# Both mixer tails as one stage per tile, with layer norm's sums over channel chunks on GpSimd

## The reference, cut to what matters

```python
# layer 0, after the depthwise convolution (u)
u = jax.nn.silu(layernorm(u, ln_g, ln_b))        # mean and variance over the 1024 channels
y = u @ pw2_w + pw2_b
x = x + g1 * y
# layer 1, after the scans (o = o_forward + o_backward, 4 heads of 256)
on = o * lax.rsqrt(jnp.mean(o * o, axis=-1, keepdims=True) + EPS)   # per head
x = x + g1 * ((on * head_g * jax.nn.silu(gate)) @ w_o)
# both: what the experts and the router read
h = rmsnorm(x, norm_g[i, 1]) * (1 + sc2) + sh2
g_logits, inner = h @ wg + bg, h @ wr + br       # 4 groups, 32 experts: 36 columns
```

## Time and profile before

| | us |
|---|---|
| median of 3 runs | 3279.66 |
| the profiled execution | 3279.33 |
| its span | 3277.7 |
| PE, DVE, ACT, POOL busy | 2565.8, 2039.8, 1393.5, 403.9 |
| first DMA of `conv_out` | 543.20 |
| first product of `conv_out` | 586.44 |
| last DVE instruction of `conv_out` starts | 728.41 |
| `route` of layer 0: first DMA, first maximum | 790.17, 815.90 |
| first product of `gla_output` | 2368.4 |
| `route` of layer 1: first maximum | 2541.31 |

### The profile page before, as it was taken

One profiled execution on the slowest core, in us unless ns is written; L12 is line 12 of the kernel. 1 busy time (PEld: TensorE's weight loads), 2 busy tenths in 40 slices (PEclk: granted clock), 3 DMA queues, 4 the chain that ended last, 5 costly groups with the idle time before them and its releaser, 6 DMA issues. The chain is left out here.

```text
span 3277.7 us, 41009 instructions
## 1 busy us (share of the span) xinstructions
PE 2565.8 (78%) x13258; PEld 2060.5 (63%) x13258; DVE 2039.8 (62%) x1900; ACT 1393.5 (43%) x1431; POOL 403.9 (12%) x447
## 2 busy tenths in 40 slices
PE   4587771984499999999925998968494499999980
PEld 0466661773388888888714886757482388888860
DVE  2479997545657777588353002348454688888865
ACT  0310001423356676577332113334312377777752
POOL 0000001000000101010051000055100110101004
PEclk8688895995699999999957999989796699999995
DMA  8354432114578899799473211013543599999966
GB/s 299 99 181 145 140 104 84 52 68 162 184 280 317 319 324 349 265 384 388 167 274 128 74 48 46 14 60 123 200 160 141 195 380 382 389 386 392 395 245 218
DMA packets 297487, 701.32 MB, mean 214 GB/s; under 512 B 22500, under 2 KB 49796, under 8 KB 297374
## 3 DMA queue, kind: packets, MB, share of 16 engines
q1 hardware_dynamic: 258802, 570.75, 48.3%
q0 software_dynamic: 22656, 75.60, 6.5%
q10 hardware_dynamic: 15936, 53.75, 4.3%
HBM read 610.01 MB, written 91.06 MB: 214 GB/s over the span
## 5 line engine op out<-in xcount | busy, mean ns | idle before, releaser
L1388 DVE TENSOR_TENSOR moe_w_lo<-moe_w_raw,moe_w_hi 128x2048 fp32r<-128x2048 f32 x384 | 862.0, 2286 | 83.6 <-ACT moe_w_hi L1317 47.5
L1317 ACT ACTIVATE moe_w_hi<-moe_w_raw 128x2048 fp32r<-128x2048 f32 x384 | 713.9, 1908 | 58.4 <-issue 37.9
L99 PE MATMUL moe_pg<-moe_w_hi,moe_xt_hi 128*128 128x512 f32 x592 | 243.9, 412 | 11.2 <-DVE moe_xt_lo L1399 5.9
L99 PE MATMUL moe_py<-moe_w_hi,moe_at_hi 128*128 128x512 f32 x592 | 241.9, 409 | 11.8 <-DVE moe_w_lo L1388 8.2
L100 PE MATMUL moe_pg<-moe_w_lo,moe_xt_hi 128*128 128x512 f32 x592 | 237.1, 401 | 0.0
L101 PE MATMUL moe_pg<-moe_w_hi,moe_xt_lo 128*128 128x512 f32 x592 | 237.0, 400 | 0.0
L100 PE MATMUL moe_py<-moe_w_lo,moe_at_hi 128*128 128x512 f32 x592 | 235.4, 398 | 0.0
L101 PE MATMUL moe_py<-moe_w_hi,moe_at_lo 128*128 128x512 f32 x592 | 234.9, 397 | 0.0
L101 PE MATMUL moe_pu<-moe_w_hi,moe_xt_lo 128*128 128x512 f32 x592 | 234.6, 396 | 0.0
L99 PE MATMUL moe_pu<-moe_w_hi,moe_xt_hi 128*128 128x512 f32 x592 | 234.4, 396 | 0.0
L100 PE MATMUL moe_pu<-moe_w_lo,moe_xt_hi 128*128 128x512 f32 x592 | 234.4, 396 | 0.0
(11 more groups left out here) (311 smaller groups left out, 5599.7 us busy)
## 6 DMA issues: line engine op xcount, KB each, us to landing
moe_w_raw<-in_moe_w SPq DMA_DIRECT2D x384, 1024.0 KB, 9.9
taps_ada_w<-in_ada_w SPq DMA_DIRECT2D x40, 1024.0 KB, 6.9
scratch_experts_out<-moe_y ACTq DMA_DIRECT2D x57, 512.0 KB, 6.4
norm_x<-scratch_residual SPq DMA_DIRECT2D x28, 512.0 KB, 3.3
scan_v<-scratch_gla_values SPq DMA_DIRECT2D x20, 512.0 KB, 4.1
scratch_experts_in<-norm_h POOLq DMA_DIRECT2D x18, 512.0 KB, 3.0
comb_x<-scratch_residual SPq DMA_DIRECT2D x18, 512.0 KB, 5.5
ada_w<-in_ada_w SPq DMA_DIRECT2D x4, 2048.0 KB, 29.2
```

Of the source, the lines that this page charges most:

```text
L99: pe.matmul(out, xh, wh, start=start, stop=False)
L1317: act.activation(hi[m][:, cut, :], raw[m][p][:, cut, :], ACT.Copy).then_inc(s(f"{m}_hi{h}"), 1)
L1388: dve.tensor_tensor(lo[m][:, cut, :], raw[m][p][:, cut, :], hi[m][:, cut, :].bitcast(F32), ALU.subtract).then_inc(s(f"{m}_lo{h}"), 1)
```

## The change

`conv_out` and `gla_output` now do per tile what `normalise` and the first part of `route` did, and those are gone from behind them. Both are written out over the tiles without hardware loops, as a software pipeline: iteration n works on the front of tile n+2, the product of tile n, the residual and norm of tile n-1 and the logits of tile n-2. `x` of a tile is normalised while it lies in SBUF; `h` is transposed and split for one tile at a time, and the logits are computed with the tokens stationary and the 36 router columns moving, so that they come out with tokens on partitions and are kept in `lg`, in the order that `route` wants. The slots of the raw weights serve as `y` and `h` once the weights are split. The stores of `x` and `h` are issued by SP. In `conv_out` GpSimd adds the 8 chunks (4+4, 2+2, 1+1) of `vt` and of its square, and PE does one product with the 1/1024 matrix for each. `dev`, `sq` and Silu work in place on `vt`, with one `sq` buffer. `route` only loads its five tables and starts with the first maximum. The diff, cut:

On GpSimd and PE in `conv_out`:

```diff
+                def over_chunks(src, dst, name):
+
+                    if added[0]:
+                        pool.wait_ge(s("halved"), added[0])
+                    pool.tensor_tensor(quads[:, :, :], src[:, 0:KC // 2, :], src[:, KC // 2:KC, :], ALU.add)\
+                        .then_inc(s("halved"), 1)
+                    pool.wait_ge(s("halved"), added[0] + 1)
+                    pool.tensor_tensor(pairs[:, :, :], quads[:, 0:2, :], quads[:, 2:4, :], ALU.add)\
+                        .then_inc(s("halved"), 1)
+                    pool.wait_ge(s("halved"), added[0] + 2)
+                    pool.tensor_tensor(dst[:, :], pairs[:, 0, :], pairs[:, 1, :], ALU.add).then_inc(s(name), 1)
+                    added[0] += 2
+
+                def total_of(t):
+                    if t not in tiles:
+                        return
+                    if t >= 2:
+                        pool.wait_ge(s("mean"), t - 1)
+                    over_chunks(vt[:, :, cols(t)], total[t % 2], "totalled")
+
+                def power_of(t):
+                    if t not in tiles:
+                        return
+                    pool.wait_ge(s("squared"), t + 1)
+                    if t >= 2:
+                        pool.wait_ge(s("var"), t - 1)
+                    over_chunks(sq, power[t % 2], "powered")
...
+                for n in range(-2, TILES):
+                    if n < 0:
+                        weight(4 * (n + 2) + 1)
+                    power_of(n + 2)
+                    if n < 0:
+                        weight(4 * (n + 2) + 3)
+                    total_of(n + 3)
 
             @block.tensor
             def _(pe):
-                def average(what, b, i, t0):
-
+                pe.wait_ge(s("mean_w"), 16)
+
+                def mean_of(t):
+                    if t not in tiles:
+                        return
+                    if t:
+                        pe.wait_ge(s("root"), t)
+                    pe.wait_ge(s("totalled"), t + 1)
+                    pe.matmul(mean, mean_w[:, :], total[t % 2][:, :], start=True, stop=True).then_inc(s("mean"), 1)
+
+                def variance_of(t):
+                    if t not in tiles:
+                        return
+                    pe.wait_ge(s("powered"), t + 1)
+                    pe.matmul(var, mean_w[:, :], power[t % 2][:, :], start=True, stop=True).then_inc(s("var"), 1)
...
+                def route_scores(t):
+                    if t not in tiles:
+                        return
+                    pe.wait_ge(s("ht_lo"), t + 1)
+                    if t == 0:
+                        pe.wait_ge(s("router_ready"), 2)
+                    else:
+                        pe.wait_ge(s("lg"), t)
+                    for k in range(KC):
+                        last = product3(pe, logits[:, 0:router.WIDTH], ht.hi[:, k, :], ht.lo[:, k, :],
+                                        router.w.hi[:, k, :], router.w.lo[:, k, :], k == 0, k == KC - 1)
+                    last.then_inc(s("scored"), 1)
+
+                for n in range(-2, TILES + 2):
+                    mean_of(n + 2)
+                    product(n, 0)
+                    variance_of(n + 2)
+                    route_scores(n - 2)
+                    product(n, 1)
+                    turn(n - 1)
```

ACT and DVE in `conv_out`:

```diff
+                for n in range(-2, TILES + 2):
+                    if n < 0:
+                        for k in range(2):
+                            weight(4 * (n + 2) + k)
+                    square(n + 2)
+                    if n < 0:
+                        for k in range(2, 4):
+                            weight(4 * (n + 2) + k)
+                    if n == 0:
+                        router.high(act)
+                    rms(n - 1)
+                    root_of(n + 2)
+                    silu(n + 2)
+                    row_high(n - 1)
+                    act_high(n + 2)
 
...
+                for n in range(-2, TILES + 2):
+                    bias_in(n - 1)
+                    deviation(n + 2)
+                    row_low(n - 2)
+                    residual(n - 1)
+                    if n < 0:
+                        for k in (0, 2):
+                            weight(4 * (n + 2) + k)
+                    act_low(n + 1)
+                    if n == 0:
+                        router.low(dve)
+                        dve.wait_ge(s("tables"), 16 * 9)
+                        for st in (CTX, LAT):
+                            dve.scalar_tensor_tensor(scale[:, st, :], scale[:, st, :], 1.0, gain[:, :],
+                                                     ALU.add, ALU.mult).then_inc(s("scale_ready"), 1)
+                        dve.wait_ge(s("scale_ready"), 2)
+                    norm(n - 1)
+                    spread(n + 2)
+                    keep_logits(n - 2)
+                dve.wait_ge(s("lg"), TILES)
         ph.close()
 
```

SP in `conv_out`, and in `route` SP's tables with the start of DVE:

```diff
+                    load_x(t)
+                router.load(sp)
+                for t in tiles:
+                    sp.wait_ge(s("x_ready"), t + 1)
+                    sp.dma_start(d.xs[t * P:(t + 1) * P, :], x[t % 2][:, :]).then_inc(s(f"x_stored{t % 2}"), 16)
+                    sp.wait_ge(s("h_ready"), t + 1)
+                    sp.dma_start(d.hd[t * P:(t + 1) * P, :], h[t % 2]).then_inc(s(f"hd_stored{t % 2}"), 16)
+                    if t + 2 in tiles:
+                        load_x(t + 2)
...
+                for dst, src in ((iota[:, :], d.iota), (before[:, :], d.before), (ones[:, :], d.ones),
+                                 (token[:, :], d.token), (next_e[:, :], d.next_expert)):
                     sp.dma_start(dst, src).then_inc(s("loaded"), 16)
...
+                dve.wait_ge(s("loaded"), 80)
                 first_max(lg[:, :, 0:GROUPS], GROUPS, gm[:, :], gsel[:, :, :])
```

`gla_output`: SP's start, then PE, ACT and DVE:

```diff
+                load_o(0)
+                sp.dma_start(head_g[:, :], d.head_g[0, :].partition_broadcast(P)).then_inc(s("head_g"), 16)
+                sp.dma_start(ident[:, :], d.ident).then_inc(s("ident"), 16)
                 weights.load(sp)
...
+                def turn_h(t):
+                    if t not in tiles:
+                        return
+                    pe.wait_ge(s("h_ready"), t + 1)
+                    pe.wait_ge(s("ot_lo"), min(t + 3, LAT_TILES))
+                    if t:
...
+                for n in range(-1, LAT_TILES + 2):
+                    product(n, 0)
+                    turn_o(n + 1)
+                    route_scores(n - 2)
+                    product(n, 1)
+                    turn_h(n - 1)
...
+                for n in range(-2, LAT_TILES + 1):
+                    if n == -2:
+                        for k in range(2):
+                            weight(k)
+                    head_root(n + 2)
+                    if n == -2:
+                        for k in range(2, 6):
+                            weight(k)
+                    rms(n - 1)
+                    ot_high(n + 1)
+                    if n == -1:
+                        for k in range(6, KC):
+                            weight(k)
+                    if n == 0:
+                        router.high(act)
+                    row_high(n - 1)
 
...
+                for n in range(-2, LAT_TILES + 2):
+                    gated(n - 1)
+                    row_low(n - 2)
+                    residual(n - 1)
+                    front(n + 2)
+                    norm(n - 1)
+                    if n == -2:
+                        weight(0)
+                    head_norm(n + 2)
+                    if n == -2:
+                        weight(2)
+                        weight(4)
+                    ot_low(n + 1)
+                    if n == -1:
+                        weight(6)
+                    if n == 0:
...
+                    keep_logits(n - 2)
```

More of the change, by code:

```diff
@@ L704, in _ @@
[L704 to L712 removed]
+                sp.dma_start(gain[:, :], d.norm_g[0, 1, :].partition_broadcast(P)).then_inc(s("tables"), 16)
@@ L714, in _ @@
+                for b in range(2):
+                    sp.wait_ge(s(f"x_stored{b}"), 16 * (TILES // 2))
+                    sp.wait_ge(s(f"hd_stored{b}"), 16 * (TILES // 2))
             @block.gpsimd
             def _(pool):
[L716 to L722 removed]
@@ new lines, in rms @@
+                def rms(t):
+                    if t not in tiles:
+                        return
+                    act.wait_ge(s("x_ready"), t + 1)
+                    if t == 0:
+                        act.wait_ge(s("scale_ready"), 2)
+                    act.activation(junk[:, :], x[t % 2][:, :], ACT.Square, accum_out=stat[:, t, 0:1])\
+                        .then_inc(s("x_squares"), 1)
+                    act.wait_ge(s("x_squares"), t + 1)
+                    act.activation(stat[:, t, 1:2], stat[:, t, 0:1], ACT.Sqrt, bias=eps[:, :], scale=1.0 / D)\
+                        .then_inc(s("x_root"), 1)
@@ new lines, in root_of, with silu @@
+                def root_of(t):
+                    if t not in tiles:
+                        return
+                    if t == 0:
```

(45 more changed lines are left out.)

741 lines of the change are left out of this document (413 added, 328 removed).

## The result

Four runs of each kernel on the same chip: 3235.73 us (3232.44 to 3238.05) against 3279.62 us (3277.10 to 3281.59), a ratio of 0.9866, 95% interval 0.9849 to 0.9883. The changed kernel is faster by 43.9 us. The forecast was 3200 with a range of 3165 to 3240; the time is inside, near the end that rival 2 had described (3236), and the gain is 55% of the one forecast.

A forecast was written before the change was run, and what follows sets the result against it. The prediction took a loop over the engines (18.2 us a tile) to bound layer 0's changed tail and TensorE (16.0) layer 1's: 3279.3 - 49.7 (layer 0) - 29.0 (layer 1) = 3200.6, forecast 3200 us, range 3165 to 3240.

The forecast's parts named there:

- rival 2: Both tails: all contention in the chain (+15 us) and PE's clock at 0.91 (+21 us), 3236 us; chance 0.17.
- Forecast -29.0: Layer-1 tail: PE sets 16.0 us a tile; route's first maximum at 2512.3 instead of 2541.31.
- the 5 us allowed: Layer-1 start: gain and loss from reordered loads cancel within 5 us, so the first product stays at 2368.4.
- Both loops then come to 18.2 us: Layer-0 steady tile: loops of 15.9 (DVE, ACT) and 15.2 (through PE), plus 2.3 us of GpSimd contention, give 18.2.
- The likeliest case: The forecast itself: 3200 us with 18.2 us a layer-0 tile, own range 3185 to 3220, chance 0.60.
- The signs of being wrong: Either stage: tile over 21 us, steady clock under 0.9, first product later than 580, or changed experts-stage length.
- the table for the square root can't be loaded earlier: Layer-0 tile: ScalarE's 1.28 us Sqrt table load must stand in the loop, since the Silu table was in.
- The two near-PE iterations: Layer-0 drain: once the front is empty, two iterations run near PE's 15 us each, row_high(8) at 746.
- The two nearly cancel in the tile's time: Layer 0: GpSimd's adds lengthen the tile about as much as the 3.3 us of matmuls they take off PE.
- 1 (3175): Layer 0: PE alone sets the tile, GpSimd's adds falling into DVE's waits; 15.9 us a tile, 3175 us; chance 0.16.
- 3 (in a row, 33.5 a tile): Layer 0: PE's 15.5 and the chain's 18 us run one after the other; 3307 us, slower; chance 0.05.
- 4 (code): Unrolled loops: instruction supply starves PE by over 5 us a tile over 15 tiles, gain gone, 3279; chance 0.02.

The follow-up runs named there:

- e4: Kernel before with only the layer-1 tail fused with its norm and scores, layer 0 left as before: 3251.9 us.
- e3: Changed kernel plus 9 discarded 128-column products per layer-0 tile in TensorE's wait ahead of the variance product: 3219.5 us.
- e2: Changed kernel with GpSimd's adds undone: TensorE adds the eight chunks, 8 products each for mean and variance in layer 0: 3214.5 us.
- e1: Changed kernel with one line moved: layer 0's router scores of tile n-2 issued ahead of the variance product of tile n+2: 3208.7 us.
- e6: e5 with ScalarE's square-root table loaded right after each tile's square in layer 0: 3205.4 us.
- e11: e10 plus 11, 17 and 11 discarded products in TensorE's three waits behind layer 0's last product: 3183.5 us.
- e10: e9 plus the early square-root table load, and TensorE adding the means of tiles 0 to 2 and variances of 0 and 1: 3187.0 us.
- e5: e1 with the 24 narrow router products spread, six after each of the first half product's last four chunks: 3204.5 us.
- e7: e1 with GpSimd's six adds a tile issued by VectorE instead, same shapes: 3201.2 us.
- e9: e5 and e7 together, on the changed kernel: mixed scores and the adds on VectorE: 3197.2 us.

## Why the prediction was half right

**Layer 1, right, with some luck.** Forecast -29.0, measured -28.1, and 27.5 alone in e4. The tile is 15.6 us where 16.0 were worked out, with PE busy throughout; the scores are 0.111 us apart where 0.12 was taken from a 256-column neighbour. The first product stood 1.3 us earlier in its stage than before, within the 5 us allowed. What the prediction did not have is that a tile here, too, can lose 1.5 us to the clock; the changed kernel's trace had one such tile, and other traces of the same stage had up to five (22.7 us gained instead of 28.1).

**Layer 0, the stages that go: right.** Norm and route's front disappeared as computed. Five small loads stand between the last logits (790.85) and route's maximum: 4.6 us, forecast 4.8.

**Layer 0, the steady tile: the term that was mis-sized.** The step "Both loops then come to 18.2 us" carried 109 us for six tiles; they took 128.4 (bias rows 611.79 to 740.16), 19.2 us more, two thirds of the miss. The mechanism in it holds: through PE the loop is 17.7 us (e3). By its own terms the prediction had that loop at 17.5 (15.2 + 2.3), not at 18.2. What the sum lacked is the clock. The prediction assumed a PE at full speed with 2.7 us of slack a tile, without asking where the slack lies. It lies in one piece, ahead of narrow products, and PE paid for it with 3.15 us at half clock (e3 against the changed kernel) in every tile, and with 1.6 us more in two of the six. The likeliest case kept the clock at 1.00, and only rival 2 had a sagging one, with a reason (all contention in the chain) and a size (1.4 a tile) that were both off; that its 3236 is the measured time is luck. The signs of being wrong that the prediction named for this stage all appeared: 21.4 us a tile on average, a clock of 0.84, and a first product at 582.07.
Of the contention itself the total was well taken (2.3 us) and its place was not: VectorE's rows lengthen by 1.8 us a tile (13.76 against 11.94 in e2), and GpSimd's sum of squares by 2.7 us (4.9, where 2.2 were estimated; with no neighbour it takes 2.6). The loop over VectorE and ScalarE, which the prediction put at 18.2 as well, is at most 16.9 in e1. That the table for the square root can't be loaded earlier was wrong: e6 loads it right behind the tile's square, and the tile becomes 0.6 us shorter.

**Layer 0, start and drain.** row_high(0) ended at 613.8, forecast 607 (+6.7): the first product began at 582.07 instead of 574, since GpSimd's queue interleaves the sums with its weights; without the sums it began at 575.40 (e2). The last iteration, from row_high(8)'s end at 773.2 to the last logits, took 17.9 us, forecast 15 (+2.9), because the last turn and 24 scores ran at half clock; e11 gives 3.3 back. The two near-PE iterations, 31.1 for 30, add 1.1. 6.7 + 19.2 + 1.1 + 2.9 - 0.4 (behind the logits) = 29.5, against 29.3 between 766.2 and 795.5; the forecast's own terms, 761 + 1.3 + 3.5, add up to 765.8.

**The adds.** "The two nearly cancel in the tile's time", the prediction said of GpSimd's adds and the products they replace. In the order as written they do not: e2 without them is 21 us faster than the changed kernel. By the Trainium skill (GPSIMD Engine Reference, 4.1 Engine selection) they belong on VectorE, and here the measurement agrees: 1.5 us against 4.9 for one sum, VectorE's time nearly unchanged. I had read the rule as lengthening the tile, because I counted the adds but not the collisions that they take along.

**Rivals.** 1 (3175): in the measured order, no. PE alone does set the tile in e10, at 3187, but there VectorE does the adds and the scores are mixed in; that is not the rival's reason. 3 (in a row, 33.5 a tile) and 4 (code): nothing of them; PE at 15.63 of 15.63 us in layer 1 is unrolled code.

## What to carry to other kernels

When an engine is to be the bound, ask not only how much slack a tile has but where it lies: on TensorE, 2.2 us in one piece ahead of short work cost 3.15 us more in clock, and reordering two lines brought the tile from 20.9 to 16.9 us. Products that wait for nothing belong in such a gap, and in layer 0 narrow products did better spread among wide ones than issued in a run. Work moved to an idle engine whose instructions hold up those of a busy one is to be priced with the lengthening of both (here 2.3 us for one sum on GpSimd and 1.8 us a tile on VectorE); and where two limits lie close together, an edit that removes one shows little until the other is gone too (e5 and e7 against e9). Mixing the scores was tried in layer 0 alone; in layer 1, where the traces show one to five slow tiles, it is open.

## What I had not expected of the hardware

- TensorE, busy without a gap, still fell to half clock behind 24 products of 36 columns in a row (e1: 655.5 to 659.2 us, so in each of the six steady tiles), and did not in any steady tile where the same products stood in four groups of six between wide ones (e5, e6, e9, e10, e11: clock 1.00). The run of 24 doesn't bring a fall each time: none in two tiles of six in e2 and in two in e7, none in most tiles of e3, behind the discarded products. In layer 1, behind 8 transposes, the same code fell in one tile of the changed kernel (2440.06 to 2457.22, 17.16 us at clock 0.90) and in one to five tiles of the other traces. What tells these apart stays open.
- A product of 36 columns behind a full weight load costs 0.111 us at full clock and 0.214 at half.
- The three small adds of a sum (512, 256, 128 elements) lie beside VectorE's instructions and take 1.86 + 1.59 + 1.31 us on GpSimd; with no neighbour they took 1.26 + 0.72 + 0.45 (in the stage's start, 545.50 to 548.10, 2.6 us in all).
- The start of the layer-0 stage moves by some microseconds from kernel to kernel with nothing changed in it: first product at 582.1, 583.5, 579.1 and 582.1 in the changed kernel, e1, e5 and e6. Together with layer 1's 183.7 to 189.1 us this makes a median difference under 4 us between two of them no evidence about a tile.
